# Modulation products and column sums of a diffusion trunk layer on 32-wide stationary blocks, with two things moved earlier

## The reference, cut to what matters

```
mod = silu(c) @ w_mod + b_mod                 # c: 2 vectors (latent, context); w_mod: 1024 x 6144
sh1, sc1, gt1, sh2, sc2, gt2 = split(mod, 6)
h = rmsnorm(x, g_mix) * (1 + sc1) + sh1
pq, pkv, pkr, hq, hf_f, hf_b, hi, hg, ga, gb = split_cols(h @ w_in)
...
o = rmsnorm(o_f + o_b, g_hg) * silu(hg)        # per head of 128 channels, 4 heads
q = rmsnorm(pq, g_q) @ w_uq ;  ckv = rmsnorm(pkv, g_kv)
...
```

## Time and profile before

| | |
|---|---|
| median of 3 runs | 2057.23 us (2057.1 to 2061.9) |
| the profiled execution's own time | 2058.16 us |
| its span in the trace | 2056.4 us |
| PE busy | 1994.0 us, 97% of the span, 13,708 matmuls |
| DVE, ACT, POOL busy | 1120.0, 766.7, 831.9 us |
| mean granted clock of PE | 0.987 of full speed |

### The profile page before, as it was taken

The page is one execution under the profiler, slowest core; times in us unless marked ns, Lnnn a source line. Parts: engine busy times, 40 slices in busy tenths (PEclk is TensorE's granted clock), DMA queues, the critical chain, the costliest instruction groups (busy, mean ns, idle before and its releaser), DMA issues.

```text
span 2056.4 us, 34056 instructions
## 1 busy us (share of the span) xinstructions
PE 1994.0 (97%) x13708; PEld 1837.9 (89%) x13708; DVE 1120.0 (54%) x1715; ACT 766.7 (37%) x1189; POOL 831.9 (40%) x595
## 2 busy tenths in 40 slices
PE   6999999999999989999999988999999999999998
PEld 5888999999999978887799877999999999988886
DVE  5314353526142047566535356988888888645363
ACT  4323233333223254767733234322222222353441
POOL 1225263535133235455535634433443443252441
PEclk9999999999999999999999999999999999999999
DMA  8563111112213284324266445422222231584661
GB/s 294 200 199 37 42 51 44 48 52 74 67 41 90 72 227 143 93 67 107 73 173 202 147 149 189 125 77 65 86 65 65 75 98 59 175 304 141 230 237 67
DMA packets 223310, 244.09 MB, mean 119 GB/s; under 512 B 57865, under 2 KB 184162, under 8 KB 223154
## 3 DMA queue, kind: packets, MB, share of 16 engines
q1 hardware_dynamic: 220962, 233.65, 37.3%
q0 software_dynamic: 2192, 8.26, 1.2%
HBM read 182.62 MB, written 59.26 MB: 118 GB/s over the span
## 4 chain that ended last, share of the span: by engine, by line
PE 53%; DVE 3%; DMA 3%; ACT 2%; POOL 1%; issue 1%; SPq 1%; DVEq 0%; ACTq 0%; POOLq 0%
PE late_psum L2938 22%; PE late_psum L2950 13%; PE late_psum L1876 4%; PE late_psum L1901 4%; PE late_psum L2897 3%; PE late_psum L2251 3%; PE late_psum L1511 1%; PE late_psum L1846 1%; DMA s_w_raw<-in_w_hg_o 1%; DVE p_lo L2056 1%; DMA scratch_extra<-e_lo 1%; DMA merge_gates<-scratch_gates 0%; DVE conv L3124 0%; ACT prob L1987 0%; PE late_psum L1515 0%
## 5 line engine op out<-in xcount | busy, mean ns | idle before, releaser
L688 PE MATMUL s_psum<-h_hi,s_w_hi 128*128 128x384 f32 x984 | 333.3, 344 | 6.4 <-DVE h_lo L1402 6.4
L688 PE MATMUL s_psum<-h_hi,s_w_lo 128*128 128x384 f32 x984 | 326.1, 337 | 0.0
L688 PE MATMUL s_psum<-h_lo,s_w_hi 128*128 128x384 f32 x984 | 325.9, 337 | 0.0
L131 POOL TENSOR_TENSOR s_w_lo<-s_w_raw,s_w_hi 128x1024 fp32r<-128x1024 f32 x41 | 100.0, 2440 | 337.0 <-ACT s_w_hi L126 337.0
L2938 PE MATMUL late_psum<-h_lo,ffn_w_hi 128*128 128x320 f32 (+1 forms) x704 | 208.5, 296 | 0.0
L2938 PE MATMUL late_psum<-h_hi,ffn_w_lo 128*128 128x320 f32 (+1 forms) x704 | 208.4, 296 | 0.0
L2938 PE MATMUL late_psum<-h_hi,ffn_w_hi 128*128 128x320 f32 (+1 forms) x704 | 208.3, 296 | 0.0
L688 PEld LDWEIGHTS s_psum<-h_hi,s_w_hi 128*128 128x128 f32 x984 | 185.5, 189 | 15.8 <-issue 14.0
L688 PEld LDWEIGHTS s_psum<-h_lo,s_w_hi 128*128 128x128 f32 x984 | 186.1, 190 | 0.0
L688 PEld LDWEIGHTS s_psum<-h_hi,s_w_lo 128*128 128x128 f32 x984 | 185.8, 189 | 0.0
L2873 POOL TENSOR_TENSOR u_lo<-u_raw,u_hi 128x384 fp32r<-128x384 f32 x66 | 112.9, 1719 | 162.5 <-ACT u_hi L2770 161.5
(11 more groups left out here) (371 smaller groups left out, 4709.9 us busy)
## 6 DMA issues: line engine op xcount, KB each, us to landing
w_raw<-in_w_ffn_out SPq DMA_DIRECT2D x66, 512.0 KB, 3.7
ffn_raw<-in_w_ffn_in SPq DMA_DIRECT2D x44, 512.0 KB, 5.3
s_w_raw<-in_w_in SPq DMA_DIRECT2D x41, 512.0 KB, 4.3
s_w_mod<-in_w_mod SPq DMA_DIRECT2D x8, 2048.0 KB, 8.3
scratch_u<-conv SPq DMA_DIRECT2D x22, 576.0 KB, 3.6
u_raw<-scratch_u SPq DMA_DIRECT2D x66, 192.0 KB, 5.2
scratch_gates<-sig SPq DMA_DIRECT2D x48, 192.0 KB, 1.9
merge_gates<-scratch_gates SPq DMA_DIRECT2D x16, 576.0 KB, 4.8
```

What stands on the lines that cost most here:

```text
L131: pool.tensor_tensor(flat[0], flat[1], flat[2], ALU.subtract).then_inc(self.lo_ready, 1)
L688: return pe.matmul(slot_bank(s), weights(c)[wx][:, k, :], hx[:, k, j * CH:(j + 1) * CH], start=(k == 0 and n == 0), stop=(k == KD - 1 and ...
```

## The change

The small products swap their operands. The wide weights are now stationary, in blocks of 32 columns that go to the four column groups of the array, and the two columns of `cc` (no longer padded) move. The result lies in PSUM as columns at once, so that ACT's copies, the turning matmuls, `m_rows`, `mod_rows` and `sel` go. For a piece or a `mod` item this is 8 contraction tiles x 4 column tiles x 4 blocks = 128 matmuls in place of 8 + 4. The sums `S` and `pe_sums` are cut into 32-wide blocks as well, 36 matmuls in place of 9. A memset of two PSUM banks on DVE stands at the start, and PE's first transposes wait for it. ACT splits weight chunks 0 and 1 before the last `x_take`, not behind it. Levels 1 and 2 of `K` of head 0 stand one slot earlier.

```diff
         for t in range(TILES):
-            last = pe.matmul(psum[:, t:t + 1], self.acc[:, t * P:(t + 1) * P], self.cst.ones[:, 0:1], start=True, stop=True)
+            for a in range(0, P, BLOCK):
+                last = pe.matmul(psum[a:a + BLOCK, t:t + 1], self.acc[:, t * P + a:t * P + a + BLOCK], self.cst.ones[:, 0:1],
+                                 start=True, stop=True)
...
         for lv in range(1, LEVELS + 1):
-            at[a + lv - 1].append(("K", h, lv))
+            at[a + lv - 1 - (h == 0 and lv <= 2)].append(("K", h, lv))
...
                 sp.wait_ge(p_ps, QUARTERS)
-                sp.wait_ge(p_t, QUARTERS)
...
                     pe.wait_ge(consts_loaded, 48)
+                    pe.wait_ge(banks_clear, 1)
...
+                def columns_of(weights_m, at, to_bank, to):
+
+                    for k in range(KD):
+                        for a in range(0, P, BLOCK):
+                            cc_last[0] = pe.matmul(psum[a:a + BLOCK, to_bank, to:to + 2], weights_m[:, k, at + a:at + a + BLOCK],
+                                                   cc[:, k, :], start=(k == 0), stop=(k == KD - 1))
+
                 def piece_product(i):
                     pe.wait_ge(p_loaded[i], 32)
                     if i == 0:
                         pe.wait_ge(cc_ready, 1)
-                    else:
-                        pe.wait_ge(p_rows, i)
-                    for part in range(2):
-                        for quad in range(4):
-                            k = 4 * part + quad
-                            last = pe.matmul(psum[32 * quad:32 * quad + 32, 6, :], cc[:, k, :], pieces[i][:, k, :],
-                                             start=(part == 0), stop=(part == 1))
-                    last.then_inc(p_ps, 1)
...
+                    if i >= 2:
+                        pe.wait_ge(p_mod, i - 1)
                     for x in range(2):
                         for j in range(QK):
...
+                            columns_of(pieces[i], x * QW + j * P, 7 - i % 2, 4 * x + 2 * j)
+                    cc_last[0].then_inc(p_ps, 1)
...
-                        if c == 0 and k + 1 < QUARTERS:
-                            piece_columns(k + 1)
...
                 def mod_product(n):
                     pe.wait_ge(wm_loaded[n % 2], 16 * (n // 2 + 1))
-                    if n >= 2:
-                        pe.wait_ge(mod_row, n - 1)
-                    for i in range(2):
-                        for quad in range(4):
-                            k = 4 * i + quad
-                            last = pe.matmul(psum[32 * quad:32 * quad + 32, 6 + n % 2, :], cc[:, k, :], w_mod[n % 2][:, k, :],
-                                             start=(i == 0), stop=(i == 1))
...
                     for j in range(4):
...
+                        columns_of(w_mod[n % 2], j * P, 5, 8 * n + 2 * j)
+                    cc_last[0].then_inc(mod_ps, 1)
...
-                x_take(2 * TILES - 1)
-                take_piece(0)
                 split(0)
                 split(1)
+                x_take(2 * TILES - 1)
                 for k in range(KD):
                     split_h(k)
-                    if k < 2:
-                        take_piece(k + 1)
...
+                dve.memset(psum[:, 6:8, 0:CH], 0.0).then_inc(banks_clear, 1)
                 dve.wait_ge(vec_t, 1)
```

More of the change, by code:

```diff
@@ L454, in stage_project @@
         pieces = piece_a + [first(f"w_mod_b{i}", [P, KD, 2 * QW]) for i in range(2)]
-        m_rows = [first(f"m_rows{i}", [P, 2, QW]) for i in range(2)]
         first_end = first.at
-        last = Arena(nc, low.sig_at - 2 * NT * 4 - KD * 32 * 4)
-        cc = last("cc", [P, KD, 32])
+        last = Arena(nc, low.sig_at - 2 * NT * 4 - KD * 2 * 4)
+        cc = last("cc", [P, KD, 2])
         y = [last(f"a1_y{i}", [P, NT]) for i in range(2)]
@@ L475, in stage_project @@
         near = early("hg_near", [P, TILES, SIDE])
-        mod_rows = [early(f"mod_rows{i}", [P, 512]) for i in range(2)]
-        sel = early("mod_sel", [P, 8])
         ostat = early("ostat", [P, 2 * TILES])
         lbt = early("lbt", [P, 24])
-        assert early.at <= low.sig_at - 2 * NT * 4 - KD * 32 * 4
+        assert early.at <= low.sig_at - 2 * NT * 4 - KD * 2 * 4
         over = Arena(nc, early_end)
@@ L502, in stage_project @@
         rot_ready = sems("rot_ready")
-        sel_step, wm_loaded = sems("sel_step"), [sems(f"wm_loaded{i}") for i in range(2)]
+        wm_loaded, banks_clear = [sems(f"wm_loaded{i}") for i in range(2)], sems("banks_clear")
         consts_loaded, ones_set, vec_t, vec_cols = sems("consts_loaded"), sems("ones_set"), sems("vec_transposed"), sems("vec_columns")
-        cc_clear, silu_ready, cc_ready, lb_exp, lb_step = sems("cc_clear"), sems("silu_ready"), sems("cc_ready"), sems("lb_exp"), sems("lb_step")
+        silu_ready, cc_ready, lb_exp, lb_step = sems("silu_ready"), sems("cc_ready"), sems("lb_exp"), sems("lb_step")
         x_loaded, sq_done, x_std, x_rstd = [sems(f"x_loaded{t}") for t in range(TILES)], sems("x_sq"), sems("x_std"), sems("x_rstd")
@@ L508, in stage_project @@
         xt_dve, xt_act = sems("x_t_by_dve"), sems("x_t_by_act")
-        p_loaded, p_ps, p_rows = [sems(f"piece_loaded{i}") for i in range(4)], sems("piece_product"), sems("piece_rows")
-        p_t, p_mod, p_gain = sems("piece_columns"), sems("piece_mod"), sems("piece_gain")
+        p_loaded, p_ps = [sems(f"piece_loaded{i}") for i in range(4)], sems("piece_product")
+        p_mod, p_gain = sems("piece_mod"), sems("piece_gain")
         h_y, h_hi_ready, h_lo_ready = sems("h_y"), sems("h_hi_ready"), sems("h_lo_ready")
-        mod_ps, mod_row, modt_ps, mod_ready, gain_done = (sems("mod_product"), sems("mod_row_ready"), sems("mod_transposed"),
-                                                          sems("mod_ready"), sems("gain_done"))
+        mod_ps, mod_ready, gain_done = sems("mod_product"), sems("mod_ready"), sems("gain_done")
         masks_loaded, state_loaded = sems("masks_loaded"), sems("state_loaded")
@@ L882, in item @@
                         for t in range(TILES):
-                            last = pe.matmul(psum[:, S_BANK, t:t + 1], osq[:, t * P:(t + 1) * P], cst.ones[:, 0:1],
-                                             start=True, stop=True)
+                            for a in range(0, P, BLOCK):
+                                last = pe.matmul(psum[a:a + BLOCK, S_BANK, t:t + 1], osq[:, t * P + a:t * P + a + BLOCK],
+                                                 cst.ones[:, 0:1], start=True, stop=True)
                         last.then_inc(s_ps, 1)
@@ L976, in item @@
                 def item(kind, h, lv):
[L977 to L981, removed]
                     if kind == "K":
@@ L1070, in x_take @@
                                    psum[:, n % 6, :].rearrange("p (k n) -> p k n", k=4), ACT.Copy).then_inc(xt_act, 1)
[L1072 to L1076, removed]
                 def split_h(k):
@@ L1087, in _ @@
                 act.wait_ge(silu_ready, 1)
-                act.wait_ge(cc_clear, 1)
-                act.activation(cc[:, :, 0:2], silu_c[:, :, :].rearrange("p g k -> p k g"), ACT.Copy).then_inc(cc_ready, 1)
+                act.activation(cc[:, :, :], silu_c[:, :, :].rearrange("p g k -> p k g"), ACT.Copy).then_inc(cc_ready, 1)
                 act.wait_ge(ones_set, 1)
-                act.activation(m_rows[1][0:1, 0, 0:8], cst.eps[0:1, :], ACT.Sqrt)
+                act.activation(y[1][0:1, 0:8], cst.eps[0:1, :], ACT.Sqrt)
                 for t in range(TILES):
@@ L1172, in _ @@
                         pool.memset(cst.eps[:, :], EPS).then_inc(ones_set, 1)
-                        pool.memset(cc[:, :, :], 0.0).then_inc(cc_clear, 1)
                 w.split_lo(pool, 0, 0)
@@ L1377, in mod_quarter @@
                 def mod_quarter(i):
-                    dve.wait_ge(p_t, i + 1)
+                    dve.wait_ge(p_ps, i + 1)
                     a = QK * i
@@ L1431, in _ @@
                         if kind == "mod_t" and h == MODS - 1:
-                            dve.wait_ge(modt_ps, MODS)
+                            dve.wait_ge(mod_ps, MODS)
                             dve.tensor_tensor(cst.mod[:, 2 * KD:6 * KD, :], psum[:, 5, 0:8 * MODS].rearrange("p (j g) -> p j g", g=2),
```

25 lines of the change are left out of this document (2 added, 23 removed).

## The result

The changed kernel takes 2095.7 us (median of 4 runs, 2092.7 to 2096.8) against 2057.2 us before (median of 4). The ratio is 1.0185, with a 95% interval of 1.0159 to 1.0212: 38 us slower. The forecast was 2041.5, its range ended at 2060, and slower had 0.15.

What follows compares the result with a forecast made beforehand. PE, busy 97% of the span, was taken to bound the kernel. Start -5.1, first chunks -3.9, items -1.1 and sums -6.2 gave -16.3 us, so 2041.5 us, with a range of 2032 to 2060.

Steps and rivals of the forecast that it cites:

- The price of a small block: In the new small matmuls, a pass of a 32-wide block costs 9.5 ns, with bounds 8 and 27.5.
- The floor of about 25 ns: For small matmuls on PE, starts at least 25 ns apart, total about 2090; the no-overlap rival had chance 0.07.
- the price of a burst: In pieces and modulation items, 128 matmuls (256 passes) take 2.6 us, with bounds 2.2 and 7.0.
- the first rival: On PE's bursts, instructions come too slowly: 0.8 us more on each of 11 bursts, +9, 2050; chance 0.20.
- The 4 us of products between bursts: In slots with items, 4.16 us of full products give time to refill instructions and speak against a clock fall.
- start: Up to the first product: earlier splits and no copy or turning let PE start at 37.8, not 42.85; -5.1 us.
- first chunks: From first product to the end of the first chunks: 31.9 us, with 1.8 for a clock fall, not 35.85; -3.9.
- items: Eight modulation items: a burst of 2.6 us replaces turning and product of 2.74 us; -1.1 us.
- sums: Column sums of four heads and two norms: 0.89 us each in place of 1.93; -6.2 us.
- The clock: Rival: PE's clock falls in slots with items, 4.3 us each; likeliest 2054, all eight 2076; chance 0.20.
- K: Levels of K of head 0 one slot earlier: PE waits nowhere for a level, so 0 us.
- The low end of the range: 2032, reached if the 4.7 us of PE's issue waits at L835 do not recur.

Runs made afterwards that it cites:

- items_64_wide: The changed kernel with the modulation items on 64-wide blocks and two column groups, 256 instructions an item in place of 512: 2086.1 us, ratio 1.0135.
- burst_probe: The kernel before with five extra bursts of 32 to 512 small matmuls behind late slots, results unread: 2104.1 us in one execution.
- items_spread: The changed kernel with each modulation item's 128 small matmuls spread over its slot, 16 after every third product: 2115.8 us, ratio 1.0285.

## Why the prediction was wrong

**The price of a small block** (9.5 ns a pass) was right: 256 passes without a gap take 2.62 us at 106.99, against 2.6. The floor of about 25 ns from start to start that the Trainium skill states (TensorE: Matmul & The Clock Gate, Back-to-back issue gap) does not hold for blocks on four column groups. That its total, about 2090, is near the measured one is chance.

**The step that failed** is the one that turned this price into the price of a burst: "A burst of 128 matmuls (256 passes) is then 256 x 0.0095 + 0.2 = 2.6 us". It leaves out how the instructions arrive. I had the mechanism as the first rival, with 0.20, and priced it at 0.8 us a burst with 1.9 as the upper end, from the 1.2 us that a packet's transfer takes. The rows show 17.9 us of gaps at the eight items, up to 3.6 each, and 5.3 at the start: the turn from one packet to the next is 3.5 to 3.8 us, and 6.75 beside bulk loads. I took the transfer (0.9 to 1.5 us in all but one packet of this stage) for the whole, and let the longest burst of the kernel before (72 passes) stand as evidence for one of 256. The 4 us of products between bursts were no help beyond one packet: with the packet that ended at 100.94 us PE had what it needed for them, the next one started only at 105.90, and an item uses two.

By the prediction's own terms: start, -5.1 forecast, +5.4 measured (48.28 for 42.85); first chunks, -3.9 forecast, +7.2 measured (42.92 us from the first product to slot 6, for 35.76, with gaps of 2.65 and 2.25 and a mean clock of 0.77); items, -1.1 forecast, +33.7 measured; sums, -6.2 forecast, -6.7 measured.

**The clock** was a rival of its own, with 0.20, as if it could only come in place of the first. They came together: the clock fell at each of the eight items, 16.7 us on top of 19.5 of gaps. `items_64_wide` shows that it falls without a gap too, and the probe that a burst of 256 passes with a short gap doesn't always bring a fall. What share of the 16.7 us the gaps have, and what share the stretches of narrow work, the runs don't separate. "4.16 us of full products between any two bursts" was no protection.

**The start.** ACT's and POOL's part held: split early, `gain_mix` 0.16, affine 2.05, alone worth 6 to 8 us against the 5.1 forecast with piece 0's turning in it. The burst of piece 0 was late by the gap of 5.33, so the low part came at about 42.4 in place of 37.8. The other 5.9 us to the first product at 48.28 are piece 1, with its gaps of 4.86 and 1.57; the prediction has no term for it.

**The sums**: -6.2 forecast, 6 x 1.12 = 6.7 by the rows. **K**: 0, and 0. **The low end of the range**, the stall at L835, was real, but it did not go by shifting the program (it grew to 7.8 us); it goes when the scattered stores do.

## What to carry to other kernels

Count instructions as well as nanoseconds: where small matmuls run back to back, price them by the packets of the instruction queue (here 128 passes per 3.5 us or more), unless the burst fits into what is already there. Cut a product into column blocks where the bursts are short (72 passes: a gain), and leave the wide operand moving where they would be long. A gap marked issue on the bounding engine is worth a look at what lies in the DMA queues, scattered stores above all; and behind each long run of such blocks look at the granted clock before anything else.

## What the hardware showed unexpectedly

- PE's instructions come 256 at a time. In `burst_probe` 146 to 225 passes run free, and then 128 passes start every 3.5 to 3.8 us (23 GB/s of traffic in all); at the start of the changed kernel, beside 340 GB/s, it was 6.75 us.
- The Trainium skill (Advanced Engine Details and Errata, ISA Cache) has lines of 16 KB, 256 instructions, and only two of them, though it also gives 128 KB for TensorE, which would be eight. The first free run was 139 to 256 passes in ten of the changed kernel's eleven bursts with a start of their own (109 in one, with only 0.18 us of gap behind it), which agrees with one line in use and one ahead, and not with eight.
- PE can be busy in 90 of 92 us and have a clock of 0.52: three wide products in turn with 32 passes of two columns.
- Going from full products into 32-wide blocks and back costs about 0.26 us a time, an estimate from the 1.08 us of a group in `items_spread`.
- 4096 elements of 4 bytes, stored by SP, cost PE about 10 us, half of it clock: they held up one packet on the instruction queue for 5.2 us.
